# The opening of a two-layer block: the first modulation block in two halves of 256 columns, with three weight tiles between them

## What is computed

```
c_act = silu(c)
mod   = c_act @ ada_w + ada_b            # c has 2048 numbers, ada_w is 2048 x 6144
shift, scale, gate = mod[:2048], mod[2048:4096], mod[4096:]
h     = rms_norm(x, pre_gain) * (1 + scale) + shift
proj  = h @ w_in                         # the first large product
```

## Time and profile before

| | |
|---|---|
| median of three runs | 2241.63 us |
| profiled execution | 2238.54 us |
| span of its records | 2236.9 us |
| TensorE busy | 2189.5 us, 98% |
| VectorE busy | 1558.6 us, 70% |
| ScalarE busy | 1107.0 us, 49% |
| first W tile on TensorE | 46.20 us after the span's start |

### The profile page before, as it was taken

How to read it: one execution, slowest core, us unless ns; L and a number is a source line. 1 busy time by engine, 2 the same in 40 slices (tenths; PEclk the granted TensorE clock), 3 DMA queues, 4 the chain that set the end, 5 groups by cost and what they waited for, 6 DMA issues and landing times.

```text
span 2236.9 us, 41095 instructions
## 1 busy us (share of the span) xinstructions
PE 2189.5 (98%) x15436; PEld 1896.0 (85%) x15436; DVE 1558.6 (70%) x2393; ACT 1107.0 (49%) x1747; POOL 104.2 (5%) x94
## 2 busy tenths in 40 slices
PE   6999999999999999999999999999999999999997
PEld 6998888888888888898888878888888888888887
DVE  6875787787887678587666667665566575566666
ACT  3444544555543465465445455554444454445454
POOL 0000000000000010120000003000000000000203
PEclk7999999999999999999999999999999999999999
DMA  9995454445544576655543335555555555555552
GB/s 381 385 348 185 163 176 162 153 153 168 171 154 164 183 249 228 202 191 191 188 142 130 125 132 202 184 183 185 180 194 188 187 171 197 186 187 181 183 182 85
DMA packets 116082, 424.90 MB, mean 190 GB/s; under 512 B 13200, under 2 KB 13456, under 8 KB 115696
## 3 DMA queue, kind: packets, MB, share of 16 engines
q1 hardware_dynamic: 111744, 407.46, 53.0%
q0 software_dynamic: 4208, 15.60, 2.1%
HBM read 414.62 MB, written 8.39 MB: 189 GB/s over the span
## 4 chain that ended last, share of the span: by engine, by line
PE 92%; DVE 4%; ACT 2%; issue 1%; DMA 0%; SPq 0%; DVEq 0%; ACTq 0%
PE ps L2150 46%; PE ps L2151 23%; PE ps L2261 5%; PE ps L2530 3%; PE ps L2206 2%; PE ps L2207 2%; PE ps L2208 2%; PE ps L2531 1%; DVE wlo L1291 1%; PE ps L2683 1%; PE ps L2190 1%; ACT whi L716 1%; DMA xt<-in_x 0%; DVE t L1504 0%; PE ps L2182 0%
## 5 line engine op out<-in xcount | busy, mean ns | idle before, releaser
L2150 PE MATMUL ps<-acts,whi 128*128 128x512 f32 x3312 | 1200.4, 405 | 3.7 <-DVE wt L1297 1.3
L1291 DVE TENSOR_TENSOR wlo<-raw,whi 128x1024 fp32r<-128x1024 f32 x629 | 784.8, 1257 | 561.3 <-ACT whi L716 559.0
L716 ACT ACTIVATE whi<-raw 128x1024 fp32r<-128x1024 f32 x671 | 703.3, 1057 | 681.0 <-PE ps L2151 596.2
L2151 PE MATMUL ps<-acts,wlo 128*128 128x256 f32 x3312 | 926.5, 280 | 0.0
L2150 PEld LDWEIGHTS ps<-acts,whi 128*128 128x128 f32 x3312 | 621.2, 188 | 163.4 <-issue 9.9
L2151 PEld LDWEIGHTS ps<-acts,wlo 128*128 128x128 f32 x3312 | 625.1, 189 | 4.6 <-issue 3.4
L2150 PE MATMUL ps<-hidn,whi 128*128 128x512 f32 x1280 | 454.7, 400 | 2.0 <-DVE s L1297 1.7
L2151 PE MATMUL ps<-hidn,wlo 128*128 128x256 f32 x1280 | 358.2, 280 | 0.0
L2150 PEld LDWEIGHTS ps<-hidn,whi 128*128 128x128 f32 x1280 | 240.3, 188 | 65.8 <-DVE s L1297 4.0
L2151 PEld LDWEIGHTS ps<-hidn,wlo 128*128 128x128 f32 x1280 | 241.5, 189 | 0.5 <-issue 0.5
L716 ACT ACTIVATE half<-ps 128x256 f32<-128x256 f32 x333 | 125.3, 382 | 59.9 <-PE ps L2151 50.5
(11 more groups left out here) (337 smaller groups left out, 2035.0 us busy)
## 6 DMA issues: line engine op xcount, KB each, us to landing
raw<-in_stream SPq DMA_DIRECT2D x767, 512.0 KB, 3.9
gate_dram<-stage POOLq DMA_DIRECT2D x32, 128.0 KB, 2.6
gab<-gate_dram POOLq DMA_DIRECT2D x8, 512.0 KB, 6.6
xt<-in_x SPq DMA_DIRECT2D x1, 2048.0 KB, 9.2
xt<-in_x POOLq DMA_DIRECT2D x1, 2048.0 KB, 9.2
ple_dram<-pr__111 POOLq DMA_DIRECT2D x4, 512.0 KB, 3.6
pj<-ple_dram POOLq DMA_DIRECT2D x1, 2048.0 KB, 11.8
out<-y__143 SPq DMA_DIRECT2D x2, 512.0 KB, 2.8
```

The source lines that it names most:

```text
L716: return nc.scalar.activation(dst, src, ACT.Copy)
L1291: tt(wlo[:, n % SPLIT, :], raw[:, in_stream(g) % RAW, :], whi[:, n % SPLIT, :].bitcast(F32), ALU.subtract).then_inc(raw_used, 1)
L2150: mm(ps[bank + n][:, :], whi[:, n0 % SPLIT, c:c + P], act[:, off + kt + k, :], start=kt + k == 0, stop=False)
L2151: ins = mm(ps[bank + n][:, 0:T], wlo[:, n0 % SPLIT, c:c + P], act[:, off + kt + k, 0:T], start=False, stop=kt + k == last)
```

## The change

The first block of 512 columns becomes two blocks of 256 columns (`ROWS`: chunks 0 to 2, 2 to 4, then 4 to 8, 8 to 12, 12 to 16). The `ada_w` tiles of these two are laid out anew: a tile of 128x1024 now holds two groups of 128 rows for 256 shift and 256 scale columns, so that each half block needs 8 tiles in place of 16, and VectorE uses such a tile with two instructions on 128x512, the second after the first. The first window is now 8 tiles (7 A, 1 P). A new window of 11 tiles follows (6 A, 2 P, 3 W), and its three W tiles need the first half block alone. Then come the three windows of 28 as before. The numbers of tiles are as before, 64 of `ada_w` and 42 W; 6 in place of 8 of the first are P tiles. The first six W tiles are put in another order, so that the first three are of chunks 0 and 1 and the next three of chunks 2 and 3. TensorE keeps one W tile waiting in the new window and three in the others (`LAG`). `vec` gets a semaphore of its own, `x` is loaded ahead of `con`, and the first P tile no longer waits for the root of the norm.

```diff
-FIRST = "AAAAAAAAPPAPAPPA"
-WITH_ADA = "AAAA" + 6 * "AW" + "PAW" + 2 * "AAW" + "WWW"
-TAIL = 3
+ROWS = ((0, 2), (2, 4), (4, 8), (8, 12), (12, 16))
+WINDOWS = ("AAAAAPAA", "WWAWAPAAPAA") + 3 * ("AAAA" + 6 * "AW" + "PAW" + 2 * "AAW" + "WWW",)
+LAG = (1, 3, 3, 3, 3)
...
+TILES = [(blk_, 2 * q + x, at) for blk_, q, at in UNITS for x in range(2)]
+TILES[:6] = TILES[0:6:2] + TILES[1:6:2]
...
-            sp.dma_start(vec[:, :], vec_in).then_inc(s.loaded, 16)
+            sp.dma_start(vec[:, :], vec_in).then_inc(s.vec_in, 16)
+            sp.dma_start(xt[:, :, :], x_in).then_inc(s.loaded, 16)
             sp.dma_start(con[:, :], con_in).then_inc(s.loaded, 16)
-            sp.dma_start(xt[:, :, :], x_in).then_inc(s.loaded, 16)
...
-            for b in range(4):
+            for b, (lo, hi) in enumerate(ROWS):
+                tiles = [(g, w) for kind, g, w in opening(b) if kind == "W"]
+                if b == 0:
+                    opened_hi(*tiles.pop(0))
+                    opened_hi(*tiles.pop(0))
                 act.wait_ge(s.mod_done, b + 1)
...
             def ada(b, g, j, prior):
+                lo, hi = sums_at(b)
+                n = hi - lo
                 dve.wait_ge(raw_ready[g % RAW], 16 * (g // RAW + 1))
...
+                for x in range(CW // n):
+                    v, row, last = raw[:, g % RAW, x * n:(x + 1) * n], j * CW // n + x, x == CW // n - 1
+                    if prior is None and x == 0:
+                        ins = ts2(acc[:, lo:hi], v, cact[:, row:row + 1], None, ALU.mult)
+                    else:
+                        if x == 0:
+                            dve.wait_ge(raw_used, taken(prior))
+                        ins = stt(acc[:, lo:hi], v, cact[:, row:row + 1], acc[:, lo:hi], ALU.mult, ALU.add)
+                    if last:
+                        ins.then_inc(raw_used, 1)
+                    else:
+                        V.step(ins)
...
-                if g == 8:
-                    dve.wait_ge(s.rms_done, 1)
-                    V.step(nc.vector.reciprocal(rs[:, :], rs[:, :]))
-                    rows_scaled(0)
-            for b in range(4):
+            dve.wait_ge(s.rms_done, 1)
+            V.step(nc.vector.reciprocal(rs[:, :], rs[:, :]))
+            rows_scaled(0)
+            for b, (lo, hi) in enumerate(ROWS):
                 prior = None
-                if b == 3:
+                if b in (0, 4):
                     modulation(b)
...
-            pe.wait_ge(s.rms_done, 1)
-            for g, j in [(g, j) for kind, g, j in opening(-1) if kind == "P"]:
-                modulated(g, j, g == FIRST.index("P"))
+            for kind, g, j in opening(-1):
+                if kind == "P":
+                    modulated(0, g, j, True)
             waiting = []
-            for b in range(4):
+            for b in range(len(ROWS)):
...
                     if kind == "W":
                         waiting.append((g, m))
-                        if len(waiting) > TAIL:
+                        if len(waiting) > LAG[b]:
                             opened_tile(*waiting.pop(0))
```

More of the change, by code:

```diff
@@ L56 @@
          (6, 3, 0), (7, 3, 1), (0, 3, 2))
-OPENED = 2 * len(UNITS)
+TILES = [(blk_, 2 * q + x, at) for blk_, q, at in UNITS for x in range(2)]
+TILES[:6] = TILES[0:6:2] + TILES[1:6:2]
+OPENED = len(TILES)
 REST = ((1, 2), (2, 2), (3, 4), (4, 4), (5, 6))
[L59 to L62, removed]
+PREVIOUS = [max((v for v in range(w) if TILES[v][2] == TILES[w][2]), default=None) for w in range(OPENED)]
+STARTS = [w for w, v in enumerate(PREVIOUS) if v is None or TILES[v][0] != TILES[w][0]]
+ENDS = [w for w in range(OPENED) if w not in PREVIOUS or PREVIOUS.index(w) in STARTS]
+OPEN = "".join(WINDOWS)
+OPEN += "W" * (OPENED - OPEN.count("W"))
 BYPE = OPEN.count("P")
@@ L184, in lay_out @@
     opened = []
-    for b in range(-1, 4):
+    for b in range(-1, len(ROWS)):
         for kind, _, n in opening(b):
-            opened.append((w_a[UNITS[n // 2][0], 2 * UNITS[n // 2][1] + n % 2] if kind == "W" else shift_scale[b + 1][n])[None])
+            opened.append((w_a[TILES[n][:2]] if kind == "W" else shift_scale[b + 1][n])[None])
     starts = [0] + [g + 1 - WB0 for g in GATE_AFTER]
@@ L234, in opening @@
 def opening(b):
-    at = 0 if b < 0 else len(FIRST) + len(WITH_ADA) * b
-    kinds = FIRST if b < 0 else OPEN[at:at + len(WITH_ADA)]
-    ada = tile = 0
+    at = sum(len(kinds) for kinds in WINDOWS[:b + 1])
+    kinds = WINDOWS[b + 1] if b + 1 < len(WINDOWS) else OPEN[at:]
+    ada, tile = 0, OPEN[:at].count("W")
     for n, kind in enumerate(kinds):
-        yield kind, at + n, WITH_ADA.count("W") * b + tile if kind == "W" else ada
+        yield kind, at + n, tile if kind == "W" else ada
         ada, tile = ada + (kind != "W"), tile + (kind == "W")
@@ L759, in part_out @@
             def part_out(w):
-                u = (w - SPLIT) // 2
-                if w % 2 == 0 or u not in ENDS[:-1]:
+                end = w - SPLIT
+                if end not in ENDS[:-1]:
                     return
-                blk_, _, at = UNITS[u]
-                act.wait_ge(quarters, used(WA0 + 2 * u + 1))
+                blk_, _, at = TILES[end]
+                act.wait_ge(quarters, used(WA0 + end))
                 for n in range(2):
@@ L778, in _ @@
                     copy(acts[:, c:c + 2, 0:T], scr0[:, c:c + 2, :]).then_inc(s.acts_hi, 2)
[L779 to L784, removed]
+                for g, w in tiles:
+                    opened_hi(g, w)
             for w in range(OPENED, OPENED + AHEAD):
@@ L1331, in rows_lo @@
[L1331 to L1334, removed]
+                lo, hi = ROWS[b]
+                n = hi - lo
+                V.do(tt(mod[:, KT + lo:KT + hi], ps[6][:, n:2 * n], vec[:, V_ADAB + KT + lo:V_ADAB + KT + hi], ALU.add))
+                V.step(tt(mod[:, lo:hi], ps[6][:, 0:n], vec[:, V_ADAB + lo:V_ADAB + hi], ALU.add))
@@ L1336, in rows_scaled, with rows_lo @@
+                stt(gpre[:, lo:hi], mod[:, KT + lo:KT + hi], 1.0, vec[:, V_PRE + lo:V_PRE + hi], ALU.add, ALU.mult).then_inc(s.mod_done, 1)
+            def rows_lo(c):
+                dve.wait_ge(s.acts_hi, c + 2)
+                tt(acts[:, c:c + 2, T:2 * T], scr0[:, c:c + 2, :], acts[:, c:c + 2, 0:T].bitcast(F32), ALU.subtract).then_inc(s.acts_ready, 2)
             def rows_scaled(b):
-                V.do(tt(scr0[:, 4 * b:4 * b + 4, :], xt[:, 4 * b:4 * b + 4, :], rs4, ALU.mult))
-                V.wait()
+                lo, hi = ROWS[b]
+                V.step(tt(scr0[:, lo:hi, :], xt[:, lo:hi, :], rs4[:, 0:hi - lo, :], ALU.mult))
@@ L2221, in _ @@
                     pe.wait_ge(s.mod_done, b)
-                for n in range(8):
-                    ins = mm(ps[6][:, n:n + 1], acc[:, b * CW + n * P:b * CW + (n + 1) * P], ones[:, 0:1], start=False, stop=n == 7)
+                lo, hi = sums_at(b)
+                for n in range((hi - lo) // P):
+                    ins = mm(ps[6][:, n:n + 1], acc[:, lo + n * P:lo + (n + 1) * P], ones[:, 0:1], start=False, stop=lo + (n + 1) * P == hi)
                 ins.then_inc(s.mod_ps, 1)
```

71 lines of the change are left out of this document (39 added, 32 removed).

## The result

The kernel after the change takes 2250.53 us (median of six runs, 2248.36 to 2253.37) against 2241.96 for the kernel before in the same series. The ratio is 1.0041 with a 95% interval of 1.0030 to 1.0053. The forecast was 4 us faster; it is 9 us slower. The profiled execution took 2250.07 us, its span is 2248.4.

A forecast was written before the change was run, and what follows sets the result against it. TensorE, busy 98% of the span, was taken as the bound. 65.57 less the P tile's new start at 61.4 gave 4.2 us: 2241.63 - 4.2 = 2237.4 us, forecast's own range 2235.5 to 2240, overall 2232.5 to 2243.

The forecast's parts named there:

- the sum: Opening up to the first long window's P tile: 65.57 less its new start at 61.4, a gain of 4.2 us.
- Past that P tile I count nothing: After the first long window's P tile (56.90 before): no further gain or loss, 0 us.
- Rival 3: Tile 21's load takes 8.6 us, not 4.4; nothing gained, or slower by 3 (2244.6 us); chance 0.10.
- The first W tile: New window on TensorE: W tile 0 starts at 28.8 us, against 46.20 before.
- The stop of the stream at tile 21: Tile 21's buffer waits for P tile 13: load issued at 38.4, landing 4.4 us later at 42.8.
- VectorE's chain: After tile 21: modulation from 44.0, gpre 44.3, remainder 46.4, wlo 3 done 49.4, W tile 3 at 49.6.
- tile 35: First long window's P tile: lands at 60.7, the stream ending last by 0.4 or 2.4 us; taken as 61.4.
- the half of a slip: Stream between tiles 21 and 35: one slip adds 1.15 us; half taken, moving the P tile's start to 61.4.
- the clock of W tiles 3 to 5: Ahead of the first long window's P tile: 10.7 us at half clock or 8.67 at full; does not matter.
- my signs of being wrong: W tile 0 after 31, P tile without a wait before 59, or TensorE waiting at the next two P tiles.
- Rival 1: At the first long window's P tile the stream doesn't hold TensorE: gain of 6, 2235.6 us; chance 0.20.
- rival 2: Stream doesn't catch up in later windows, TensorE waits 3 us more: gain 1.2, 2240.4 us; chance 0.18.

The follow-up runs named there:

- e1: Kernel after, but W tiles 12, 13, 36 and 37 multiplied with rows of h already there, same work and order: 2240.48 us, 0.9986 to before.
- e2: Kernel after with 10 W tiles in place of 12 in the first long window: 2240.18 us, 0.9983 to before.
- e8: e5 with con loaded ahead of x: 2240.48 us, 0.9978 to before.
- e5: e2 with the new window's two P tiles moved, one to its start, one to its end: 2241.36 us, 0.9981 to before.
- e9: e8 with the P tile of each of the three long windows summed by VectorE instead: 2236.31 us, 0.9964 to before.

## Why the prediction was wrong

The step that failed is in the sum: "Past that P tile I count nothing", and before it, "Past it both programs give TensorE the same work, less these three." The work is the same, the order against the modulations is not. I shifted the list of W tiles by three against the windows and kept the number that waits, and did not ask which tiles those are and what they need. This term stood at nothing. The waits that take the cover's place are 4.3 and 3.2 us, and with the sums and the clock behind them they cost 10.9 us by the ledger. e1, which takes that away, came 12 us under the kernel after by its ratio (0.9986 for 1.0041) and 10 by its median (2240.48 for 2250.53). None of my rivals held it. Rival 3, the only slower one, asked for a load of 8.6 us; it took 3.7.

The other steps, one by one. The first W tile was forecast for 28.8 and came at 29.98; 0.9 of the 1.2 is the stream's later start (tile 0 at 13.2 for 12.3), which varies as much between runs of one order of loads. The two W tiles took 7.9 us for 7.8, and the two P tiles behind them were done at 41.5 where 40.0 was worked out; 1.2 of that is the later start, and the clock was full under them (1.00 from 34.8 to 41.4). The stop of the stream at tile 21 was right (issue 39.75 for 38.4, landing 43.5 for 42.8), and so was VectorE's chain (W tile 3 at 50.8 for 49.6). The stream did end last at tile 35: 62.85, with a wait of 1.66, for 61.4 and 0.5 to 2.5. The gain up to there is 2.7 for 4.2; the later start of the stream (0.9) and the half of a slip that I had left out make up the difference. That the clock of W tiles 3 to 5 does not matter was true, since the P tile waited for the stream all the same; the clock behind the P tile did matter, with 1.5 us, and I had not counted it. With cover the change gains about what the sum had: by the ratios e1 is 3.1 us and e2 3.8 us faster than before, and the openings of their profiles are shorter by 3.0 and 1.8.

None of my signs of being wrong came, neither a late W tile 0, nor a P tile without a wait, nor waits at the next two P tiles. They all watched the stream. What showed the miss was the line that said "no other wait until 170".

Rival 1 did not occur in this kernel: the stream held TensorE by 1.66 us. Of rival 2 the mechanism (TensorE waiting at the next P tile) shows in e8 alone.

## What to carry to other kernels

When work is pulled ahead in a pipelined order, look up for each later wait which instructions stand behind it after the shift, and what they need. A queue of fixed length that hides a latency does so only as long as its members belong to the finished part, and pulling three tiles ahead used up exactly the three that hid it. In a stretch where the stream and the engine run at nearly the same pace, let no step need a transfer at the moment that it lands: a single slip of the stream then becomes a wait, as in e5.

## What the runs showed of the hardware

The stream's slips have a visible companion. In the kernel before, tiles 17, 37, 48, 57, 69 and 92 landed 0.8 to 1.2 us behind the pace of 1.28 a tile, and within the 3 us ahead of each lies one packet of 16 KB of the instruction queue (q8). These packets come 13 to 28 us apart. From 60.2 to 62.5 us, where tile 37 lands 0.9 late, the DMA queues have these packets, MB and shares:

```profile
q1 hardware_dynamic: 234, 0.84, 98.5%
q8 instruction: 1, 0.02, 2.9%
q14 instruction: 1, 0.01, 0.9%
```

The share of 2.9% of 16 engines over 2.3 us is 1.07 us of one engine. If a tile needs a part from every engine, one engine's delay is the tile's; no row here shows the engines apart. In e5 such a packet (2.3% of 2.9 us) lies in the stretch from 58.8 to 61.7 where tile 35 lands 1.6 late. That it is the cause was not tried. In the kernel before, one such packet, at 120.4, has no late tile behind it, and in the kernel after some tiles are late by as much with no packet near, such as tile 23 by 0.95.

The lower clock came behind waits of 1.0 us (e8) and 1.7 us (the kernel after) at a P tile, and lasted 6.9 and 3.4 us. In both, one-column matmuls stood next to the wait; TensorE had such matmuls and a wait too in the 19.4 us at 0.50 from 26.8 to 46.2 of the earlier trace rows. The Trainium skill, "TensorE: Matmul & The Clock Gate", section "HAM oscillation — how this bites in real kernels", tells of such falls behind waits for DMA. The traces agree in these two places. But they do not make a rule of it: in e9 the clock stayed full behind 1.1 us of waiting and the sums at 73.69, and in e5 it fell for 3.4 us at 98.3 with no such wait ahead. The wait in e9, and the stretch in e5 (columns as in the earlier trace rows):

```profile
73.69 0.27 PE L2254 MATMUL ps<-con,acc 128*128 128x1 f32 x1 [1.08 <-DVE acc L1343]
```

```profile
98.30:101.60 3.30, 3.30 (x18) 3.30 (x17) 3.30 (x4) 2.03 (x3) 0.00 (x0) 0.50 1.02 406
```

What decides between these cases stays open.
